# A decoder step with one chain of hand-ordered engines: page rows, first product, first queries, memory keys and state moved

## The reference

```
h  = rmsnorm(x) @ w_in                         # 3352 columns, x is 1024 wide
o_n = g0*cmp(q_n) + g1*slc(q_n) + g2*win(q_n)  # 8 query heads: compressed, selected, window keys
o_r = groupnorm(retention(rope(q_r), rope(k_r), v_r))  # 4 heads, also returns the new state
o_m = softmax(q_m k_m / 8) v_m                 # 4 heads, 256 memory tokens
y  = rmsnorm(x + (concat(o_n, o_r, o_m) * silu(z)) @ w_out)
# prompt: k_m, v_m = rmsnorm(mem) @ w_mem_kv; sample: k_m, v_m from cache_mem
# sample: compressed and selected keys are pages of a pool, picked through page_table
```

## Time and profile before

| | us |
|---|---|
| median of 3 runs | 1098.66 (1098.10 to 1100.58) |
| the profiled execution | 1095.08 |
| its span | 1093.3 |
| TensorE busy in it | 988.1 |
| VectorE, ScalarE, GpSimd busy | 512.1, 390.4, 209.5 |

### The profile page before, as it was taken

The page is one execution under the profiler, slowest core; times in us unless marked ns, Lnnn a source line. Parts: engine busy times, 40 slices in busy tenths (PEclk is TensorE's granted clock), DMA queues, the critical chain, the costliest instruction groups (busy, mean ns, idle before and its releaser), DMA issues.

```text
span 1093.3 us, 20913 instructions
## 1 busy us (share of the span) xinstructions
PE 988.1 (90%) x8117; PEld 853.2 (78%) x8117; DVE 512.1 (47%) x1241; ACT 390.4 (36%) x961; POOL 209.5 (19%) x318
## 2 busy tenths in 40 slices
PE   1999999999999999998767888989898998999994
PEld 1999999999999999898555566666665776768883
DVE  4763332322225433362346557666655657634432
ACT  4432221142110121133335455555555557632210
POOL 1122221311152455412002012020010232002000
PEclk9999999999999999999689899999999999999997
DMA  7453431432425333173634484240330133013430
GB/s 197 158 196 101 143 114 62 143 76 95 128 71 138 110 116 102 35 175 103 158 108 123 139 271 114 56 156 1 91 98 1 52 97 128 18 49 125 147 123 38
DMA packets 100675, 119.15 MB, mean 109 GB/s; under 512 B 38770, under 2 KB 82706, under 8 KB 100002
## 3 DMA queue, kind: packets, MB, share of 16 engines
q1 hardware_dynamic: 88962, 78.44, 25.3%
q0 software_dynamic: 8704, 32.43, 8.5%
q10 hardware_dynamic: 2912, 6.95, 1.8%
HBM read 92.72 MB, written 32.02 MB: 114 GB/s over the span
## 4 chain that ended last, share of the span: by engine, by line
PE 69%; DVE 8%; issue 7%; DMA 5%; ACT 5%; SPq 3%; POOL 2%; ACTq 0%; DVEq 0%; POOLq 0%
PE psum L501 10%; PE psum L502 9%; PE psum L503 9%; PE psum L1500 4%; PE psum L1623 4%; PE psum L1473 3%; DVE p_nb L1798 3%; PE psum L1639 3%; PE psum L1640 3%; PE psum L1641 3%; ACT p_P L1722 2%; PE psum L1474 2%; PE psum L723 2%; PE psum L725 2%; PE psum L724 2%
## 5 line engine op out<-in xcount | busy, mean ns | idle before, releaser
L501 PE MATMUL psum<-a_whi,f_xhi 128*128 128x256 f32 (+2 forms) x968 | 279.8, 289 | 0.0
L502 PE MATMUL psum<-a_wlo,f_xhi 128*128 128x256 f32 (+2 forms) x968 | 274.2, 283 | 0.0
L503 PE MATMUL psum<-a_whi,f_xlo 128*128 128x256 f32 (+2 forms) x968 | 273.3, 282 | 0.0
L501 PEld LDWEIGHTS psum<-a_whi,f_xhi 128*128 128x128 f32 (+1 forms) x968 | 178.2, 184 | 2.7 <-issue 0.9
L502 PEld LDWEIGHTS psum<-a_wlo,f_xhi 128*128 128x128 f32 (+1 forms) x968 | 178.2, 184 | 0.0
L503 PEld LDWEIGHTS psum<-a_whi,f_xlo 128*128 128x128 f32 (+1 forms) x968 | 178.1, 184 | 0.0
L1722 ACT ACTIVATE p_P<-psum,p_nb 128x640 f32<-128x640 f32 (+7 forms) x224 | 123.8, 557 | 138.9 <-DVE p_nb L1798 128.5
L638 POOL DMA_DIRECT2D h_scratch<-a_hst x117 | 64.5, 553 | 262.5 <-DVE a_hst L940 176.8
L1500 PE MATMUL psum<-f_ident,p_P 128*128 128x128 f32 (+1 forms) x656 | 108.3, 285 | 5.9 <-DVE p_QB L1891 4.8
L1798 DVE TENSOR_REDUCE p_nb<-psum 128x1 f32<-128x640 f32 (+7 forms) x224 | 109.7, 520 | 4.3 <-PE psum L1476 3.3
L1661 DVE COPY p_PT<-psum 128x512 f32<-128x512 f32 (+4 forms) x108 | 56.3, 521 | 92.5 <-PE psum L1500 92.1
(11 more groups left out here) (290 smaller groups left out, 1757.8 us busy)
## 6 DMA issues: line engine op xcount, KB each, us to landing
a_wraw<-in_w_in SPq DMA_DIRECT2D x24, 512.0 KB, 5.4
h_scratch<-a_hst POOLq DMA_DIRECT2D x96, 128.0 KB, 2.1
s_SG<-in_cache_nsa_slc SPq DMA_DIRECT2D x64, 128.0 KB, 2.2
a_xraw<-in_x_prompt SPq DMA_DIRECT2D x8, 512.0 KB, 3.5
p_qd<-h_scratch SPq DMA_DIRECT2D x16, 256.0 KB, 3.9
s_MK<-in_cache_mem SPq DMA_DIRECT2D x8, 512.0 KB, 5.7
mix_scratch<-p_zt POOLq DMA_DIRECT2D x8, 512.0 KB, 3.0
s_WG<-in_cache_nsa_win SPq DMA_DIRECT2D x8, 512.0 KB, 5.8
```

Source lines behind the costliest of these rows:

```text
L501: nc.tensor.matmul(out, hi, wh, start=first, stop=False)
L502: nc.tensor.matmul(out, hi, wl, start=False, stop=False)
L503: return nc.tensor.matmul(out, lo, wh, start=False, stop=last)
```

## The change

Seven edits, all of them of place and order; no product, norm or softmax is changed.

1. POOL's page rows begin with a wait for the third tile's scaling (`x_scaled` 3).
2. SP fetches the second half of the first weights ahead of the second tile. The step `hl` (the calls of `hi` and `lo`) is taken out of `x`, and the first tile's comes at once; job (0, 0) stands ahead of the second tile's transposes, and the other jobs of chunk 0 one tile earlier.
3. The states of the sample tile are made in two parts: banks of sequences 0 to 5 in `r_o`, those of 6 and 7 (new step `r_o2`) behind the next job.
4. The first queries are transposed and split in the trunk (new step `qtr`) behind the fourth and fifth job of the last chunk, and no longer between the last job and the first scores. For that `QB0` and `QB1` change places in memory.
5. `MK` gets a second buffer (`MKs`), each half has its own semaphore, and `load_mem(1)` waits for nothing. SP's attention walk begins with the sample group's rows and `load_mem(0)`.
6. `load_z` moves from SP's walk to POOL's, for all tiles.
7. The sample group's mixing works in place (`ms` is gone).

```diff
@@ -292,7 +295,10 @@
     sg_at = ru.at
     SG = ru("SG", [128, 2, NPG, 256])
     MK = nc.alloc_sbuf_tensor_at("s_MK", [128, 4, 2, 512], F32, offset=sg_at)
+    wg_at = ru.at
     WG = ru("WG", [128, 2, 4, 256])
+    ru.at = wg_at + 4 * 2 * 512 * 4
+    MKs = [MK, nc.alloc_sbuf_tensor_at("s_MK2", [128, 4, 2, 512], F32, offset=wg_at)]
     kt_at = ru.at
     KTs = ru("KTs", [128, 2, PAST])
     KTm = nc.alloc_sbuf_tensor_at("s_KTm", [128, 4, 2, NM], F32, offset=kt_at)
...
@@ -376,17 +381,20 @@
 
         for n in range(NT + 2):
             steps.append(("x", n))
+            if n >= 2:
+                steps.append(("hl", n - 1))
             evict(0)
             if n == 0:
                 steps.append(("split", ("w", 0)))
+                steps.append(("hl", 0))
             if n == 2:
                 steps.append(("split", ("w", 1)))
             if n == 6:
                 steps.append(("split", ("c", 0)))
-            if n >= 2:
-                job(0, n - 2)
             if n >= 3:
                 job(1, n - 3)
+            if n == 0 or 2 <= n <= NT:
+                job(0, max(0, n - 1))
             if n == NT - 1:
                 steps.append(("gather", 0))
         steps.append(("x_end", 0))
...
@@ -406,10 +414,10 @@
         groups += [[], [("sec", NIDX - 1)], [("r_init", 0), ("rope", 0)], [("rope", 1)], [], [("r_t", 0)], [("r_s", 0)]]
         for n in range(NT):
             groups.append([("r_t", n + 1)] if n + 1 < NT else [("r_z", 0)])
-            groups.append([("r_o", n)] + ([("load_r", n + 2), ("rope", n + 2)] if n + 2 < NT else [("r_bd_out", 0)] if n == QT - 1 else [("r_s_out", 0)]))
-            groups.append([("r_s", n + 1)] if n + 1 < NT else [("r_fin", 0), ("load_k", 0)])
+            groups.append([("r_o", n)] + ([("load_r", n + 2), ("rope", n + 2)] if n + 2 < NT else [("r_bd_out", 0)] if n == QT - 1 else []))
+            groups.append([("r_s", n + 1)] if n + 1 < NT else [("r_o2", 0), ("r_fin", 0), ("r_s_out", 0), ("load_k", 0)])
             groups.append([])
-        groups += [[], [], [], [], [("ktr", 0), ("ktr", 1)], [("ktr", 2), ("ktr", 3)], [("ktr", 4), ("maskb", 0)]]
+        groups += [[], [], [], [], [("ktr", 0), ("ktr", 1)], [("ktr", 2), ("ktr", 3)], [("ktr", 4), ("maskb", 0)], [("qtr", 0), ("qtr", 1)], [("qtr", 2)]]
         fill = []
         for j in range(2, NCH):
             tiles = (NT, NT + 1) if j in MEM_CHUNKS else range(NT)
...
@@ -522,8 +530,8 @@
         sp.dma_start(gb[:, 0, :], io["ln_mix"].to_broadcast([128, D])).then_inc(S("gain_in"), 16)
         load_raw(sp, 0)
         sp.dma_start(ident[:], io["c_ident"]).then_inc(S("ident_in"), 16)
+        load_raw(sp, 1)
         load_x(1)
-        load_raw(sp, 1)
         sp.dma_start(gb[:, 1, :], io["ln_mem"].to_broadcast([128, D])).then_inc(S("const_in"), 16)
         sp.dma_start(colc[:], io["c_col"]).then_inc(S("const_in"), 16)
         sp.dma_start(pt[:], io["page_table"].rearrange("b p -> (b p)").rearrange("(a n) -> a n", a=1)).then_inc(S("const_in"), 16)
...
@@ -597,13 +605,14 @@
         if i == 1:
             sp.wait_ge(S("p_maskb"), 1)
         if i >= 2:
-            sp.wait_ge(S("p_tr"), q_last[i - 2] + 1)
+            sp.wait_ge(S("p_tr"), q_last[i - 2] + 1) if i >= 3 else sp.wait_ge(S("q0_tr"), 3)
         for j in range(2):
             sp.dma_start(qd[i % 2][:, 0:8, j, :], hD[rows, 0:512].rearrange("p (h d) -> p h d", d=HD)).then_inc(S(f"p_q{i % 2}"), 16)
             sp.dma_start(qd[i % 2][:, 8:12, j, :], hD[rows, C_QM:C_QM + 256].rearrange("p (h d) -> p h d", d=HD)).then_inc(S(f"p_q{i % 2}"), 16)
 
     def pool_trunk(pool):
         ch = Link(pool, S("r_pool"))
+        pool.wait_ge(S("x_scaled"), 3)
         pool.dma_start(pD[:, :, 0:1], io["page_table"].rearrange("b (p o q) -> (b p) o q", o=1, q=1).to_broadcast([NDB * NPG, NPG, 1]), allow_slow_non_contiguous=True).then_inc(S("row_in"), 16)
         pool.wait_ge(S("row_in"), 16)
         pool.dma_start(rowi[0][:], pD[:, :, 0].rearrange("(u j) c -> (j c) u", u=NDB // 2), allow_slow_non_contiguous=True).then_inc(S("row_in"), 16)
...
@@ -773,6 +782,15 @@
                 r_scores(pe, n)
             elif what == "r_o":
                 r_output(pe, n)
+            elif what == "r_o2":
+                pe.wait_ge(S("r_ns"), 1)
+                r_states((6, 7)).then_inc(S("r_use"), 1)
+            elif what == "qtr":
+                pe.wait_ge(S("p_q0"), 64)
+                pe.wait_ge(S("p_klo"), 8)
+                for j in range(4):
+                    l = nc.tensor.transpose(bank(5 + n)[:, 128 * j:128 * j + 128], qd[0][:, 4 * n + j], ident[:])
+                l.then_inc(S("q0_tr"), 1)
             elif what == "ktr":
                 pe.wait_ge(S(f"p_k{n // 2}"), 16)
                 pe.wait_ge(S("r_done"), NT)
...
@@ -878,6 +896,10 @@
             elif what == "r_fin":
                 act.wait_ge(S("r_ve"), 1)
                 nc.scalar.activation(small[:, 116:152], small[:, 80:116], ACT.Sqrt).then_inc(S("r_sd"), 1)
+            elif what == "qtr":
+                act.wait_ge(S("q0_tr"), n + 1)
+                act.wait_ge(S("w_split"), 2 * len(ring))
+                nc.scalar.activation(QA[0][:, 4 * n:4 * n + 4, :], bank(5 + n).rearrange("p (j c) -> p j c", j=4), ACT.Copy, scale=SCALE).then_inc(S("q0_hi"), 1)
             elif what == "ktr":
                 act.wait_ge(S("p_ktr"), n + 1)
                 for kv in range(2):
...
@@ -922,12 +944,12 @@
                     dve.wait_ge(S("x_tr"), 2 * (n - 1))
                 nc.vector.scalar_tensor_tensor(out=xs[n % 2][0:r, :], in0=xraw[n % 2][0:r, :], scalar=small[0:r, 48 + n:49 + n],
                                                in1=gb[0:r, int(n >= NT), :], op0=ALU.mult, op1=ALU.mult).then_inc(S("x_scaled"), 1)
-                if n >= 1:
-                    lo(n - 1)
                 if n == 1:
                     dve.wait_ge(S("const_in"), 48)
                     dve.wait_ge(S("ident_in"), 16)
                     nc.vector.tensor_copy(identb[:], ident[:]).then_inc(S("identb"), 1)
+            elif what == "hl":
+                lo(n)
             elif what == "x_end":
                 lo(NT + 1)
             elif what == "split":
...
@@ -1032,14 +1061,14 @@
             pe.wait_ge(S("r_qz"), 2)
             pe.wait_ge(S("r_kvr"), QT)
             pe.wait_ge(S("r_at"), 2 * NT)
-            for b in range(NDB):
-                if b == 6:
-                    l.then_inc(S("r_kvs"), 1)
-                    pe.wait_ge(S("r_ns"), 1)
-                for pr in range(2):
-                    o2 = 512 * KV_BANKS[b // 2] + 256 * (b % 2) + 128 * pr
-                    l = nc.tensor.matmul(psum[:, o2:o2 + 128], KZ[:, b, 128 * pr:128 * pr + 128], v[0:r, 512 + 128 * pr:640 + 128 * pr], start=True, stop=True)
-            l.then_inc(S("r_use"), 1)
+            r_states(range(6)).then_inc(S("r_kvs"), 1)
+
+    def r_states(bs):
+        for b in bs:
+            for pr in range(2):
+                o2 = 512 * KV_BANKS[b // 2] + 256 * (b % 2) + 128 * pr
+                l = nc.tensor.matmul(psum[:, o2:o2 + 128], KZ[:, b, 128 * pr:128 * pr + 128], rr[QT % 2][0:NS_TOK, 512 + 128 * pr:640 + 128 * pr], start=True, stop=True)
+        return l
 
     class retention_dve:
 
...
@@ -1175,7 +1204,7 @@
         groups = [[("t", ("sq",))]]
         for g in range(2):
             groups += [[("t", ("mk", b))] for b in range(4 * g, 4 * g + 4)]
-            groups += [[("t", ("mq", g))], [("me", g)], [("t", ("mt", g))], [], [("t", ("mv", g)), ("load_mem", 1) if g == 0 else ("load_pair", 0)], [("store_mem", g)]]
+            groups += [[("t", ("mq", g))], [("me", g)], [("t", ("mt", g))], [], [("t", ("mv", g)), *([("load_pair", 0)] if g == 1 else [])], [("store_mem", g)]]
         for p in range(NPAIR):
             groups += [[("t", ("sc", p))], [("ec", p)], [("nc", p)], [], [("t", ("si", p))]]
             groups += [[("t", ("kt", p, c))] for c in (4, 5)]
...
@@ -1356,19 +1383,9 @@
         wait_stored(sp, len(proj_jobs) - 1)
         srows = hD[T:T + NS_TOK, :]
 
-        def load_z(i):
-            rows = slice(128 * i, 128 * i + 128)
-            if i >= 2:
-                sp.wait_ge(S(f"p_mxo{i % 2}"), 16 * (i // 2))
-            sp.dma_start(gt[i % 2][:], hD[rows, C_G:C_G + 24]).then_inc(S(f"p_g{i % 2}"), 16)
-            for o, c, n in ((0, C_ZN, 512), (512, C_ZR, 256), (768, C_ZM, 256)):
-                sp.dma_start(zt[i % 2][:, o:o + n], hD[rows, c:c + n]).then_inc(S(f"p_z{i % 2}"), 16)
-
         def load_mem(g):
-            if g == 1:
-                sp.wait_ge(S("p_tr"), place["mv", 0] + 1)
             for b in range(4 * g, 4 * g + 4):
-                sp.dma_start(MK[:, b % 4], io["cache_mem"][0, b].rearrange("(t p) a h d -> p t (a h d)", p=128)).then_inc(S("m_in"), 16)
+                sp.dma_start(MKs[g][:, b % 4], io["cache_mem"][0, b].rearrange("(t p) a h d -> p t (a h d)", p=128)).then_inc(S(f"m_in{g}"), 16)
 
         def load_pair(p):
```

(16 more changed lines are left out.)

59 lines of the change are left out of this document (34 added, 25 removed).

## The result

| | before | changed |
|---|---|---|
| median | 1098.38 us (1095.68 to 1100.58, 4 runs) | 1067.43 us (1066.33 to 1068.74, 4 runs) |
| span of the profiled execution | 1093.3 | 1066.4 |
| TensorE busy in it | 988.1 | 983.6 |

A forecast was written before the change was run, and what follows sets the result against it. TensorE was taken as full through the trunk, so gains lay only in its waits and half-clock work. Terms -3.5 - 2.6 + 3.2 - 13.9 - 6.4 - 5.2 = -28.4 on the 1098.66 median gave 1070.3 us, range 1062 to 1081.

The forecast's parts named there:

- Start: Kernel start, up to tile 3's transposes: earlier weights and reordered DVE steps save 3.5 us (0 to 7).
- L: Time the second half of the first weights has landed: 17.2 before, taken as 12 after the change.
- State: Sample state in the trunk: splitting it saves 2.6 us (0 to 5.0), limited by DVE's split of the last weights.
- Boundary: Trunk to attention: transposes in the trunk, POOL's gate load and the later table load cost 3.2 us (1.5 to 6).
- Memory keys: Early attention: earlier key loads and a second buffer remove PE's waits, saving 13.9 us (8 if a load is late).
- Pages: Pair 0's pages in the attention: asked for 6.4 us earlier without SP's z loads, saving 6.4 us (2.1 to 6.6).
- Clock: Attention: half-clock work behind the removed waits goes or shrinks, saving 5.2 us (1 to 8).
- The end: Behind 620: nothing the change touches is waited for, so earlier gains should last to the end; no term given.
- The loads did not collide: Rival, from 515 on: simultaneous key, query and z loads bring back a 5 us wait; 1078 us, chance 0.15.
- POOL's loads did not starve: Rival, boundary and behind: VectorE copies block POOL's descriptors, gates 3 us late, +3 and +2; 1075 us, chance 0.04.
- no drain shows at the table load: Rival, boundary: the table load costs a drain too, 1.4 us more; 1072 us, chance 0.02.
- More than forecast: Rival, whole kernel: state gives 5, L falls to 10, clock stays up from first scores; 1063 us, chance 0.10.

The follow-up runs named there:

- experiment 8: Kernel before with only the page rows' wait for the third tile's scaling added; 1090.63 us, ratio 0.9924.
- experiment 1: Changed kernel with the page rows starting at once again, without the wait for the third tile's scaling; 1075.53 us, ratio 0.9786.
- experiment 3: Changed kernel with the last two sample states following the first six at once again; 1069.06 us, ratio 0.9744.
- experiment 6: Changed kernel with the loads of gates and z (`load_z`) on SP again instead of POOL; 1075.25 us, ratio 0.9782.
- experiment 4: Changed kernel with tile 0's gates read ahead of unit 4's maximum, the exponential's table loaded early, last h stores awaited behind unit 1; 1068.69 us, ratio 0.9733.
- experiment 5: Changed kernel with experiment 4's edit, plus SP issuing the two constants and first memory-key half before waiting for the last h stores; 1070.12 us, ratio 0.976.
- Experiment 7: Changed kernel with one buffer for the memory keys again, the second half's load waiting for the first `mv`; 1077.4 us, ratio 0.9805.
- experiment 11: Changed kernel with experiment 4's edit, plus the sample group's steps beginning at unit 6 instead of 4; 1064.49 us, ratio 0.9683.

## Why the prediction was right, and where it was not

- **Start, -3.5 forecast, -7.8 measured.** The mechanism was right. The term was mis-sized in two places: L (12 taken, 9.87 measured) and the 2.4 us for half clock, which did not come. For L I gave the page rows 3 us between the bounds 0 and 6; experiment 8 has 6.3 for them alone, just above the upper bound, and experiment 1 has 6.5 in the changed kernel. The order of the loads, taken at 2.5, is worth 1.4. Seven of the 7.8 are typical (the mean of the traces with either start), so some of this was the luck of the pair.
- **State, -2.6 forecast, -2.5 measured**, bounded by DVE's chain as I said, though most of PE's waiting for it (1.51 of 1.89) stood at ACT's copy of a job and not ahead of the last chunk; experiment 3 shows the gain in the trunk. The 1.6 us in the recorded text for the products at half clock come to 1.3 by the earlier trace rows; the forecast does not use them.
- **Boundary, +3.2 forecast, +3.9 measured.** The table load behind `p_nb` (1.3) came. The gates by way of POOL cost 1.0 (experiment 6) where I had 0.4: the load is issued 3.1 us behind the last eviction (2.6 before), and used 2.2 behind its issue (1.7 before). 0.1 is left that no run assigns. The step that I missed is that none of it had to be there: the wait for the gates is only a matter of DVE's order, and it covered the sample group's loads (experiments 4 and 5).
- **Memory keys, -13.9 forecast, -13.3 measured**, in the two parts and by the two causes given. Experiment 7 gives the second part by itself (7.4 of wait); the first, the order of SP's loads, was not undone alone.
- **Pages, -6.4 forecast, -5.0 measured.** The loads came in time, but the waits for them had covered others: PE now waits 1.70 for DVE's `QB` where it had waited 2.12 for `s_WG`, and 2.2 for DVE's copy of a key window and 1.3 for ACT's of the pages, where it had waited 2.0 and 0.2. The step that I missed is to ask what else each of those places waits for. Experiment 6 brings 4.7 back, all at `s_SG`, with 1.7, 2.2 and 0.3 at the three others.
- **Clock, -5.2 forecast, +1.4 measured.** This is the step that failed. I took it that half clock follows a wait and goes with it. Experiment 7 bears that out where the wait is 7.4 us, for 0.8 us. But behind the boundary the clock stays low with the long wait or without it: 16.9 and 20.3 us in traces with it (experiment 3, the changed kernel), 17 and over 23.5 without it (experiments 4 and 11, below); why is not shown. Where the half clock behind `s_SG` did go, PE gained 2.3 us and gave 1.9 back in waits for ACT, so even there almost nothing of the 2.0 came. And short stretches come at places that differ from run to run of nearly the same code (606, 750 and 818 in experiment 4; 577 and 816 in 3), behind no wait for a transfer. What sets them was not found. The +1.4 is one pair's figure behind maximum 56; the medians leave up to 4.1 us more for the whole change, which no row places.
- **The end, nothing forecast, -3.6 measured.** Edit 6 raised the number of POOL's transfers from 145 to 177. I had costed it by its place in the queues alone.
- **Rivals.** The loads did not collide (no wait on `s_MK` or `p_qd`), POOL's loads did not starve (the gates came 0.5 us later behind their issue than from SP), but DVE was idle for 5.25 us until it read them, so that rival's condition did not arise; and no drain shows at the table load. "More than forecast" came true in one of its three conditions only, L at 10.

## What to carry to other kernels

A tiny transfer of scattered words can cost more than a big one, as the page table did here: look at what the queues move (GB/s at a high share) while it is in flight, and put it where nobody waits for a load. When a wait is taken out, list which loads were issued against the same event: they had the same lateness, covered by that wait, and they are the next one. Compare two traces by the starts of the same instructions, since a right total can hold two wrong terms, and look at several traces of the same code first, to know how far one place moves by itself. Don't count a gain from the clock unless a trace has shown it.

## What the runs showed of the hardware

- **POOL's stop.** In all twelve profiles in which POOL issues the last store, the span ends 5.3 to 5.4 us behind it where POOL had issued 177 transfers and 8.9 to 9.0 us where it had issued 145; with the last store on SP it is 3.0 to 3.1. Only these two counts were run, so whether it depends on a remainder, a fill of some ring or a threshold is open.
- **Scattered words.** 64 entries of four bytes, each written eight times (2 KB), take 8.6 us to land when issued at 21.6, and when they are issued at 1.3 the next step on POOL comes 12.4 us later (experiment 1); meanwhile the loads move a third of what they do without it (128 against 380 GB/s).
- **Half clock without a long wait.** 6.5 us at a granted clock of 0.50 directly behind 10 us at 1.00 with PE busy 9.13 of 10. And in experiment 11, behind the boundary, the clock stays at 0.50 for 23.5 us in which PE is busy 21.10:

```profile
507.50:531.00 23.50, 21.10 (x113) 16.92 (x113) 8.59 (x33) 10.26 (x42) 6.85 (x21) 0.50 1.01 291
```
